# Second output projection: strips 3 with 4 and 5 with 6 by seven block products over twelve of the sixteen rows, whose outputs are read back a second time

## What is computed

```
o = ...                                     # (512 tokens, 2048), 16 heads of 128
h = h + (o * silu(r)) @ w_out               # w_out: 2048 x 1024
y = h * rsqrt(mean(h*h, -1) + 1e-6) * g     # final norm
```

## Time and profile before

| | |
|---|---|
| median of 3 runs | 1006.11 us (1006.05 to 1006.96) |
| the profiled execution | 1006.16 us |
| its span in the trace | 1004.4 us |
| granted TensorE clock | 1.00 of full speed (0.99 in the last 24 us) |
| busy: PE / PEld / DVE / ACT / POOL | 997.5 / 938.4 / 699.2 / 541.5 / 90.5 us |
| strips 2 to 6 | 929.42 to 984.49 us in the span |

### The profile page before, as it was taken

The page is one execution under the profiler, slowest core; times in us unless marked ns, Lnnn a source line. Parts: engine busy times, 40 slices in busy tenths (PEclk is TensorE's granted clock), DMA queues, the critical chain, the costliest instruction groups (busy, mean ns, idle before and its releaser), DMA issues.

```text
span 1004.4 us, 19027 instructions
## 1 busy us (share of the span) xinstructions
PE 997.5 (99%) x7735; PEld 938.4 (93%) x7735; DVE 699.2 (70%) x1150; ACT 541.5 (54%) x903; POOL 90.5 (9%) x97
## 2 busy tenths in 40 slices
PE   9999999999999999999999999999999999999998
PEld 8999999999999999997889989999899989988887
DVE  6874677477567875436899975888589966886333
ACT  6754654564465564334576655666466645665332
POOL 0000000000000000000332212222112211200000
PEclk9999999999999999999999999999999999999999
DMA  8221231131122113333334432444245423483412
GB/s 292 73 77 64 67 102 44 63 105 65 64 77 92 44 63 127 105 110 101 114 96 107 112 132 71 121 103 153 85 104 116 137 92 91 126 265 124 148 44 84
DMA packets 40663, 104.52 MB, mean 104 GB/s; under 512 B 4592, under 2 KB 12656, under 8 KB 40576
## 3 DMA queue, kind: packets, MB, share of 16 engines
q1 hardware_dynamic: 39856, 102.63, 33.5%
q10 hardware_dynamic: 720, 0.68, 0.2%
HBM read 95.20 MB, written 7.90 MB: 103 GB/s over the span
## 4 chain that ended last, share of the span: by engine, by line
PE 90%; DVE 6%; issue 2%; ACT 1%; DMA 0%; DVEq 0%; ACTq 0%
PE psum L1876 54%; PE psum L2252 13%; PE psum L2171 7%; PE psum L2230 3%; PE psum L2001 2%; PE psum L2211 1%; DVE w_lo L1139 1%; PE psum L1949 1%; PE psum L1997 1%; PE psum L2199 1%; PE psum L2198 1%; PE psum L2200 1%; PE psum L1970 1%; PE psum L2135 1%; PE psum L1929 1%
## 5 line engine op out<-in xcount | busy, mean ns | idle before, releaser
L1139 DVE TENSOR_TENSOR w_lo<-raw,w_hi 128x1024 fp32r<-128x1024 f32 x156 | 190.5, 1238 | 41.7 <-ACT w_hi L626 31.4
L626 ACT ACTIVATE w_hi<-raw 128x1024 fp32r<-128x1024 f32 x156 | 162.9, 1052 | 31.9 <-PE psum L2171 29.5
L1876 PE MATMUL psum<-xh,w_hi 128*128 128x264 f32 x768 | 159.1, 288 | 0.3 <-DVE w_lo L1153 0.3
L1876 PE MATMUL psum<-xl,w_hi 128*128 128x264 f32 x768 | 155.9, 285 | 0.0
L1876 PE MATMUL psum<-xh,w_lo 128*128 128x264 f32 x768 | 155.3, 283 | 0.0
L1876 PEld LDWEIGHTS psum<-xh,w_hi 128*128 128x128 f32 x768 | 118.6, 189 | 1.6 <-issue 1.5
L1876 PEld LDWEIGHTS psum<-xl,w_hi 128*128 128x128 f32 x768 | 119.5, 188 | 0.0
L1876 PEld LDWEIGHTS psum<-xh,w_lo 128*128 128x128 f32 x768 | 119.1, 189 | 0.0
L576 POOL TENSOR_TENSOR sub<-sub,cst 128x128 f32<-128x128 f32 x64 | 51.4, 804 | 648.9 <-DMA sub<-sums 648.9
L1876 PE MATMUL psum<-y_lo,w_hi 128*128 128x264 f32 (+2 forms) x400 | 104.8, 314 | 0.0
L1876 PEld LDWEIGHTS psum<-y_lo,w_hi 128*128 128x128 f32 x400 | 66.7, 188 | 4.6
(11 more groups left out here) (323 smaller groups left out, 2387.7 us busy)
## 6 DMA issues: line engine op xcount, KB each, us to landing
raw<-w_all SPq DMA_DIRECT2D x143, 512.0 KB, 3.5
sub<-sums SPq DMA_DIRECT2D x16, 264.0 KB, 7.3
y_keep<-sq SPq DMA_DIRECT2D x14, 256.0 KB, 2.2
y<-y_keep SPq DMA_DIRECT2D x14, 256.0 KB, 6.5
sub<-sums SPq DMA_DIRECT2D x16, 200.0 KB, 6.2
sub<-sums SPq DMA_DIRECT2D x16, 136.0 KB, 4.9
hT<-xT SPq DMA_DIRECT2D x8, 264.0 KB, 5.7
h_keep<-hT SPq DMA_DIRECT2D x8, 256.0 KB, 4.1
```

The source lines that it names most:

```text
L626: nc.scalar.activation(w_hi[:, n % HI_RING, :], raw[:, n % LO_RING, :], ACT.Copy).then_inc(hi_made, 1)
L1139: nc.vector.tensor_tensor(w_lo[:, n % LO_RING, :], raw[:, n % LO_RING, :], w_hi[:, n % HI_RING, :].bitcast(F32), ALU.subtract).then_inc(lo ...
L1876: i = nc.tensor.matmul(o, w[a][:, k % KT, :], x[b][:, k, c0:c1], start=k == first and a == b == 0, stop=k == last and a == 1)
```

## The change

Strips 0, 1, 2 and 7 stay as they are. Strips 3 and 4 (pair 0) and 5 and 6 (pair 1) are computed together. Of the 16 rows, rows 0 to 11 form two blocks of six (`QR = 6`), tokens form two blocks of 256, and each pair's 2x2 by 2x2 block product is made of seven products of six rows by 256 tokens (`tail_product`: 18 products on PE). Rows 12 to 15 are done as before with 512 tokens (`tail_rest`: two for a pair, 12 products each). The chunks are called s00 to s06 for pair 0 and s10 to s16 for pair 1. Four of each are loaded (six rows of a block and two of the rest rows); s04, s05 and s06 hold sums only and are not loaded.

- SP reads rows 0 to 11 of `y_keep` a second time, into `yr`, before it loads w2b.
- DVE makes four sums of token blocks in place in `yr` (`tail_token_sums`), 128 x 6 x 256 values each, between the low part of w2a and the addition of strip 0. ACT makes their high parts (`t2_hi`, printed as t_hi), DVE their low parts (`yl`, in place of `yr`).
- For each pair DVE makes two weight sums (`tail_weight_sums`), 128x768 each, from the first three chunks, and POOL two more. The high part of s00 and of s10 waits for DVE's two.
- The outputs of a pair are put together by DVE in eleven additions into `hT` and `u23`, ACT copies one product (`m1`).
- PE waits for new things: before s01 and s11 for `o_made` (strip 2 or the last addition of pair 0), before s06 for the addition "4", before s10 for `u3` of pair 0.

The weights are laid out to match on the host, as before. The core of the diff:

```diff
+PAIRS, QR = (3, 5), 6
+SW = QR * P
...
+                if n == CHUNK[f"r{FOX_HEADS - 1}"] + LO_RING:
+                    done(sp, f"r{FOX_HEADS - 1}")
+                    sp.wait_ge(zhi_made, YT // 2 + 1)
+                    for r in range(2 * QR):
+                        sp.dma_start(yr[:, r, :], y_keep[r]).then_inc(y_back, 16)
...
+            for p in range(len(PAIRS)):
+                a11, a12 = (raw[:, CHUNK[f"s{p}{i}"] % LO_RING, 0:SW] for i in (2, 3))
+                if p:
+                    pool.wait_ge(lo_made, CHUNK[f"s{p - 1}6"] + 1)
+                n = CHUNK[f"s{p}2"]
+                pool.wait_ge(w_loaded[n % LO_RING], 16 * LOADS[n])
+                pool.wait_ge(sum_made, tail_sum(p, 2))
+                nc.gpsimd.tensor_tensor(s_raw[:, 1], s_raw[:, 0], a11, ALU.subtract).then_inc(sum_made, 1)
+                pool.wait_ge(w_loaded[(n + 1) % LO_RING], 16 * LOADS[n + 1])
+                pool.wait_ge(sum_made, tail_sum(p, 3))
+                nc.gpsimd.tensor_tensor(s_raw[:, 2], a12, s_raw[:, 1], ALU.subtract).then_inc(sum_made, 1)
...
+            tail_token_sum_hi(T2_HI_ORDER[0])
+            split_to("w2b")
+            tail_token_sum_hi(T2_HI_ORDER[1])
+            out_square(0, 1)
+            out_square(1, 2)
+            tail_token_sum_hi(T2_HI_ORDER[2])
+            tail_token_sum_hi(T2_HI_ORDER[3])
+            split_to("s03")
+            out_square(2, 3)
...
-            for d in range(KT - 1):
-                if d:
-                    ahead(f"w{d}a")
-                done(dve, f"w{d}")
...
+            def tail_token_sums():
+                dve.wait_ge(y_back, 16 * (NS - 1 - YT // 2 + 2 * QR))
+                tt(x12, x22, x12, ALU.subtract, t_made)
+                dve.wait_ge(t_made, 5)
+                tt(x11, x12, x11, ALU.add, t_made)
+                dve.wait_ge(t_made, 6)
+                tt(x21, x11, x21, ALU.subtract, t_made)
+                tt(x22, x22, x11, ALU.subtract, t_made)
...
+            def tail_weight_sums(p):
+                a21, a22, a11 = (raw[:, CHUNK[f"s{p}{i}"] % LO_RING, 0:SW] for i in (0, 1, 2))
+                for i in range(3):
+                    n = CHUNK[f"s{p}{i}"]
+                    dve.wait_ge(w_loaded[n % LO_RING], 16 * LOADS[n])
+                    if i == 1:
+                        if p:
+                            dve.wait_ge(sum_made, tail_sum(p, 0))
+                            dve.wait_ge(lo_made, CHUNK[f"s{p - 1}4"] + 1)
+                        else:
+                            done(dve, f"a{H - 1}")
+                        tt(s_raw[:, 0], a21, a22, ALU.add, sum_made)
+                dve.wait_ge(sum_made, tail_sum(p, 1))
+                tt(a21, a11, a21, ALU.subtract, sum_made)
...
+            tail_token_sums()
+            out_add(0)
+            split_to("w2b")
+            out_add(1)
+            tail_token_sum_lo(2)
+            out_squares_sum(1)
+            tail_token_sum_lo(3)
+            tail_weight_sums(0)
+            split_to("s01")
+            tail_token_sum_lo(0)
+            tail_token_sum_lo(1)
+            out_add(2)
+            split_to("s03")
...
+                tail_add(p, hT[:, d, META:T], "m", bank(4), "2", "m")
+                split_to(f"s{p}6")
+                dve.wait_ge(copied, NS - S0 + p + 1)
+                tail_add(p, hT[:, d, first_half], "1", m1, "m", "1")
+                both = hT[:, d:d + 2, second_half]
+                tail_add(p, both, "5", bank(5, 0, HS).rearrange("p (a n) -> p a n", a=1).to_broadcast([P, 2, HS]), "1", "5")
+                if p + 1 < len(PAIRS):
+                    tail_weight_sums(p + 1)
+                else:
+                    split_to(f"w{KT - 1}a")
+                dve.wait_ge(prod_done, tail_made(p, "6"))
+                tt(u23[:, 0], bank(6, 0, HS), m1, ALU.add, out_made)
+                dve.wait_ge(out_made, tail_output(p, "u2"))
+                tt(u23[:, 1], bank(3, 0, HS), u23[:, 0], ALU.add, out_made)
+                split_to(f"s{p + 1}0" if p + 1 < len(PAIRS) else f"w{KT - 1}b")
+                tail_add(p, hT[:, d + 1, first_half], "6", u23[:, 1], "u3", "21")
+                tail_add(p, both, "6", u23, "u3", None)
+                if p + 1 < len(PAIRS):
+                    split_to(f"s{p + 1}1")
+                dve.wait_ge(o_made, d + 1)
+                dve.wait_ge(out_made, tail_output(p, "21"))
+                tail_add(p, hT[:, d, second_half], "3", bank(2, 0, HS), None, None)
...
-            for d in range(2, KT - 1):
-                wait_slot(pe, f"w{d}")
-                out_late(d, "a", range(0, 8)).then_inc(half_done, 1)
-                out_late(d, "b", range(8, 16)).then_inc(job_done, 1)
+            wait_slot(pe, "w2")
+            out_late(2, "a", range(0, 8)).then_inc(half_done, 1)
+            out_late(2, "b", range(8, 16)).then_inc(job_done, 1)
...
+            for p in range(len(PAIRS)):
+                if p:
+                    pe.wait_ge(out_made, tail_output(p - 1, "u3"))
+                tail_product(bank(3, 0, HS), f"s{p}0", tail_x(2))
+                pe.wait_ge(o_made, 3 + 2 * p)
+                tail_product(bank(2, 0, HS), f"s{p}1", tail_x(3))
+                tail_rest(bank(7), (f"s{p}0", f"s{p}1"))
+                tail_product(bank(0, 0, HS), f"s{p}2", b11)
+                tail_product(bank(1, 0, HS), f"s{p}3", b21)
+                tail_rest(bank(4), (f"s{p}2", f"s{p}3"))
+                tail_product(bank(5, 0, HS), f"s{p}4", tail_x(0))
+                tail_product(bank(6, 0, HS), f"s{p}5", tail_x(1))
+                pe.wait_ge(out_made, tail_output(p, "4"))
+                tail_product(bank(2, 0, HS), f"s{p}6", b22)
```

More of the change, by code:

```diff
@@ L277, in program @@
                 with ExitStack() as three:
+                    t2_hi = sb("t2_hi", [P, 4, QR, HS], F32R, three)
+                    s_raw = sb("s_raw", [P, 3, SW], F32, three)
+                    with ExitStack() as four:
+                        yr = sb("yr", [P, 2 * QR, SEQ], F32, four)
+                    yl = sb("yl", [P, 2 * QR, SEQ], F32R, three)
+                with ExitStack() as three:
                     fq_hi = sb("fq_hi", [P, SEQ], F32R, three)
@@ L2432 @@
         n = int("".join(x for x in name if x.isdigit()))
-        if name[0] in "Ww":
+        if name[0] == "s":
+            d, i = PAIRS[int(name[1])] + (int(name[2]) < 2), int(name[2]) % 2
+            at = [*range(QR * i, QR * i + QR), 2 * QR + 2 * i, 2 * QR + 2 * i + 1]
+            chunks.append(np.concatenate([rows(wo2, P * k, 1, d * P, P) for k in at], axis=1))
+        elif name[0] in "Ww":
             half_rows = name[-1] == "b"
```

143 lines of the change are left out of this document (119 added, 24 removed).

## The result

| | before | after |
|---|---|---|
| median | 1006.54 us (1006.05 to 1007.27, 4 runs) | 1017.16 us (1016.72 to 1019.59, 4 runs) |
| ratio | | 1.011, 95% interval 1.0092 to 1.0127 |
| the profiled execution | 1006.16 us | 1019.59 us |
| its span | 1004.4 us | 1017.8 us |

Slower, as forecast, but by 10.6 us where 3.6 were expected; 1017.16 is outside the range of 1006.8 to 1012.5.

What follows compares the result with a forecast made beforehand. PE was taken to bound the kernel; waits of 2.83 + 1.88 + 1.63 + 0.27 = 6.61 us less 3.05 us of products gave +3.56 on 1006.16, so 1009.7 us. The range was 1006.8 to 1012.5 us.

Steps and rivals of the forecast that it cites:

- products: Strips 3 to 6 on PE: 252 short and 48 long products take 41.01 us instead of 44.06, 3.05 less.
- What bounds the kernel: PE, busy 99% of the span: a product removed shortens the kernel and a PE wait lengthens it, one for one.
- The read back: Twelve reads into `yr` before the token sums: they land by 919 us, before 924, and cost nothing.
- First wait: PE before strip 2: four token sums delay strip 0's addition, so PE waits 2.83 us.
- What lies beside other work: GpSimd's sums, ScalarE's work in pair 1 and the output additions are in time or covered, except where named.
- The clock: Rival: clock falls after the wait before strip 2, half a strip slow, costing 5.5 us: 1015.2 us; chance 0.03.
- Second wait: PE before s01, which needs bank 2 after strip 2's addition: waits 1.88 us.
- Third wait: PE before s10, whose high part awaits VectorE's sums and the third chunk's load: waits 1.63 us.
- Fourth: PE before s11, which needs bank 2 after the addition of product 3: waits 0.27 us.
- The thinnest cover: s12's low part in pair 1 ends near 974.1 us, PE wants it at 974.6: 0.5 us to spare.
- cheap vector steps: Rival: 1536-value steps before strip 0's and strip 2's additions cost less, giving 1005.0 or 1003.1 us; chance 0.07.
- late chunks: Rival: pair 1's chunk loads take 6.5 us instead of 3.3, third wait grows by 3.2: 1012.9 us; chance 0.08.

Runs made afterwards that it cites:

- early_tokens: Changed kernel with three of the four token sums moved ahead, two before and one behind head 15's last VectorE step; 1013.40 us.
- wait_4: Kernel before, with four unused VectorE sums of 128 x 1536 values added before strip 0's addition, so that TensorE waits; 1010.45 us.
- sums_dve: Changed kernel with GpSimd's two weight sums of each pair made by VectorE instead; 1010.36 us.
- pool_late: Changed kernel with GpSimd's sums started only after strip 2's addition (pair 0) or the last addition of pair 0 (pair 1); 1010.90 us.
- wait_5: Kernel before, with five unused VectorE sums of 128 x 1536 values added before strip 0's addition; 1013.15 us.
- first_a22: Changed kernel with weight sums on VectorE, token sums earlier, strip 2's addition earlier, and each pair's first two chunks swapped; 1005.53 us.

## Why the prediction was right or wrong

The sum, forecast against the trace of the changed kernel (a wait as the delay that it causes):

| term | forecast us | trace us | from |
|---|---|---|---|
| products | -3.05 | -3.3 | 252 at 0.118, 48 at 0.2295 |
| wait before strip 2 | 2.83 | 2.62 | 934.65 - 932.03 |
| wait before s01 | 1.88 | 4.13 | 952.06 - 947.93 |
| wait before s10 | 1.63 | 2.61 | 975.64 - 973.03 |
| wait before s11 | 0.27 | 1.77 | 979.60 - 977.83 |
| clock at its lower level | 0 | 2.8 | s01 4.01 instead of 2.11; 5 rest products 2.04 instead of 1.15 |
| sum | +3.56 | +10.6 | stretch 10.79, medians 10.6 |

- **What bounds the kernel** held: TensorE is the bound, every wait was paid in full, the products gave what was forecast.
- **The read back** costs nothing: the twelve reads landed in 2.9 to 5.9 us, and the four `yr` sums follow on without a wait for them, 1.75 us each.
- **First wait** right, 2.62 us for 2.83. Its cause, the four token sums, is shown by `early_tokens` (sums moved, wait gone), and its size by `wait_4` (2.8).
- **The step that failed first** is the one on GpSimd's sums under "What lies beside other work", put at nothing. The prediction asked whether their results are in time, and they are. It did not ask what VectorE does meanwhile: at that place the low parts that PE waits for. The price is 4.74 - 2.36 = 2.38 us before s01, and in pair 1 0.72 for a low part and 1.6 for two additions, with 1.0 more before s10 and 1.5 before s11 on PE. The three waits together are 4.7 us over the forecast, of the 7.0 that it was short. `sums_dve` and `pool_late` show it from two sides. GpSimd's sums of the kernel before were read as a duration of GpSimd, never as one of VectorE. Its trace did hold the price, where GpSimd's short additions (0.46 us alone) meet VectorE's low parts:

```profile
556.39 1.21 DVE L1139 TENSOR_TENSOR w_lo<-raw,w_hi 128x1024 fp32r<-128x1024 f32 x1
556.37 1.55 POOL L576 TENSOR_TENSOR sub<-sub,cst 128x128 f32<-128x128 f32 x1 [0.81 <-DMA sub<-sums]
557.52 1.48 DVE L1139 TENSOR_TENSOR w_lo<-raw,w_hi 128x1024 fp32r<-128x1024 f32 x1
```

  The two began together; GpSimd's addition took 1.55 us, and the next low part ended 1.08 us behind it, after 1.48 us instead of 1.22.
- **The clock is the second step that failed**, a term put at nothing. It was among the rivals, with 5.5 us, but behind the first wait and with a chance of 0.03. It came behind the second and cost 2.8. Against it I had nothing but that no such wait was shown, which is no evidence, and the forecast itself has two more waits of this kind. The trace of the kernel before shows one fall, at its very end: 0.92 from 1003 to 1004 us and 0.50 behind, some 4 us after TensorE's last product. `wait_4` and `wait_5` show that such a wait does it without anything else of the change. The Trainium skill, "TensorE: Matmul & The Clock Gate", section "HAM oscillation", holds that idle gaps bring the throttle back; by that rule, these traces agree, though not every gap did it (below).
- **Second wait**: without GpSimd's part the chain of fifteen steps was right: in `sums_dve` strip 2's addition starts 15.03 us behind strip 0's (946.86 - 931.83), forecast 15.04. The forecast for the whole, 1009.7, is 0.7 below what that kernel takes, though with other terms (1.7 us of clock in place of the second wait).
- **Third wait** 1.69 and 1.73 us idle in `sums_dve` and `pool_late`, 1.84 and 1.88 as delays, forecast 1.63. **Fourth**: neither of the two shows one over 0.2, forecast 0.27.
- **The thinnest cover**, s12, was the right place to point to; it came due in `first_a22`.
- **The rivals** of cheap vector steps and late chunks did not come: 1536 values cost 1.75 us, the loads of pair 1 delayed VectorE by 0.6 us in all.

The chances were too sure: 0.82 on a sum in which an operation of a third engine beside the critical chain had been given no range.

What stays open: when a wait brings the clock down and when not. It fell in or behind waits of 1.84, 2.46 (three times), 2.59, 3.34, 3.98 and 4.38 us, and it did not behind 1.00, 1.61, 1.69, 1.73 and 2.46 (twice, both in the changed kernel). So length alone does not decide it. What would settle it was not run.

## What to carry to other kernels

Where work is given to GpSimd because it is idle, look up what VectorE does at that very time. If VectorE's instruction takes both inputs from SBUF and GpSimd's reads SBUF, price the meeting with what is left of GpSimd's instruction, as VectorE's time; if TensorE waits for that step, the sums are cheaper on VectorE itself or one stage later. Add to a new wait of TensorE of about 2 us and more 1.5 to 3 us for the clock, as something that may happen: of the ten waits from 1.84 us up that are traced here, eight had a fall. And when a reordering saves work but adds waits, take the waits one by one: each one removed shows the next, and the same products that cost 10.6 us at first brought 2.9 us at the end.
